# Hybrid decoder step on 8 cores: a split first weight load, filler matmuls, and a new instruction order around the sample rows and the pass change

## What is computed

```python
xn = rmsnorm(h, g_mix); z = xn @ w_in          # x_a | B_a | C_a | u | v | g_a | g_b
y_a = (B_a * dwconv3(C_a * x_a)) @ w_out_a     # mixer A
v = rmsnorm(gelu(v), g_v); s = tril(W_s[g]) v + b_s[g]   # in chunks of 128 positions
y_b = (gelu(u) * s) @ w_out_b                  # mixer B
h += (sigmoid(g_a) * y_a + sigmoid(g_b) * y_b) @ w_o
up = dwconv3(rmsnorm(h, g_ffn) @ w_up); h += (gelu(a) * b) @ w_down
h += sigmoid(rmsnorm(h, g_ple) @ w_ple_gate) * (p @ w_ple)
y = rmsnorm(h, g_final)
```

## Time and profile before

| | us |
|---|---|
| median of 3 runs (lowest, highest) | 1170.34 (1170.22, 1171.02) |
| the profiled execution's own time | 1170.05 |
| its span on the slowest core (core 2) | 1168.3 |
| spans of the 8 cores | 1163.5 to 1168.3 |
| PE busy in the span | 1124.1 (96%) |
| DVE, ACT, POOL busy | 609.8, 384.7, 341.8 |
| granted TensorE clock of the 8 cores, share of full | 0.996 to 0.998 |
| DMA queues: share of 16 engines | 40.9% (weights), 11.3% (the rest) |

### The profile page before, as it was taken

The page is one execution under the profiler, slowest core; times in us unless marked ns, Lnnn a source line. Parts: engine busy times, 40 slices in busy tenths (PEclk is TensorE's granted clock), DMA queues, the critical chain, the costliest instruction groups (busy, mean ns, idle before and its releaser), DMA issues.

```text
span 1168.3 us, 18289 instructions; the slowest of 8 cores (1163.5 to 1168.3 us)
## 1 busy us (share of the span) xinstructions
PE 1124.1 (96%) x6425; PEld 574.5 (49%) x6520; DVE 609.8 (52%) x668; ACT 384.7 (33%) x649; POOL 341.8 (29%) x451
## 2 busy tenths in 40 slices
PE   4999999999999999999899999999999999999996
PEld 2444454444444444443446666666644444444443
DVE  3267662123687776124615866322267888871247
ACT  3622221111354444014772223112133444430134
POOL 2411113222234434114832010222223333330144
PEclk9999999999999999999999999999999999999998
DMA  7983642544844333358699355244377343343443
GB/s 185 183 158 72 111 71 46 80 83 78 145 93 72 73 73 72 62 92 192 196 195 233 63 116 90 37 73 73 72 127 127 73 73 73 73 90 64 79 102 129
DMA packets 58585, 119.77 MB, mean 103 GB/s; under 512 B 33264, under 2 KB 34032, under 8 KB 55936
## 3 DMA queue, kind: packets, MB, share of 16 engines
q0 software_dynamic: 20112, 82.85, 40.9%
q1 hardware_dynamic: 38240, 35.58, 11.3%
q10 hardware_dynamic: 144, 0.17, 0.1%
HBM read 184.14 MB, written 9.95 MB: 166 GB/s over the span
## 4 chain that ended last, share of the span: by engine, by line
PE 88%; POOL 3%; issue 2%; DVE 2%; DMA 2%; ACT 1%; DVEq 0%; POOLq 0%; ACTq 0%; SPq 0%
PE pq L322 88%; POOL s_wd L335 2%; DMA s_ring<-wpk 1%; DVE s_wd L338 1%; ACT s_xnb L329 1%; POOL s_st_r L335 1%; POOL s_st_ss L335 1%; DMA s_h<-x 1%; ACT s_wd L329 0%; DVE s_h L338 0%; PE pq L326 0%; POOL s_R L335 0%; DVE s_xnb L510 0%; DVE s_xnb L338 0%; DVE s_xn L335 0%
## 5 line engine op out<-in xcount | busy, mean ns | idle before, releaser
L322 PE MATMUL pq<-s_xn,s_ring 128*128 128x512 bf16 (+3 forms) x3693 | 658.1, 334 | 4.2 <-DVE s_wd L338 0.8
L322 PEld LDWEIGHTS pq<-s_xn,s_ring 128*128 128x128 bf16 x3744 | 335.6, 98 | 313.2 <-issue 2.0
L338 DVE SCALAR_TENSOR_TENSOR s_wd<-pq,s_cst,s_wd 128x1023 f32<-128x1023 f32 (+1 forms) x176 | 225.2, 1282 | 63.1 <-ACT s_carry_f L332 53.8
L335 POOL TENSOR_TENSOR s_R<-s_wd 128x1024 bf16<-128x1024 f32 (+3 forms) x84 | 146.3, 1742 | 357.9 <-DVE s_wd L338 166.6
L322 PE MATMUL pq<-s_ring,s_R 128*128 128x512 bf16 x936 | 206.9, 379 | 2.7 <-DVE s_wd L338 1.4
L338 DVE SCALAR_TENSOR_TENSOR s_wd<-s_wd,pq 128x512 f32<-128x512 f32 (+4 forms) x98 | 66.7, 681 | 193.2 <-PE pq L322 170.4
L329 ACT ACTIVATE s_wd<-pq 128x512 f32<-128x512 f32 (+4 forms) x138 | 78.4, 568 | 240.1 <-PE pq L322 238.7
L329 ACT ACTIVATE s_wd<-pq,s_cst 128x1024 f32<-128x1024 f32 x88 | 98.1, 1114 | 165.5 <-PE pq L322 165.5
L322 PEld LDWEIGHTS pq<-s_ring,s_R 128*128 128x128 bf16 x960 | 93.2, 98 | 112.5 <-issue 1.8
L322 PE MATMUL pq<-s_R,s_ring 128*128 128x347 bf16 (+3 forms) x875 | 125.1, 292 | 0.3
L322 PE MATMUL pq<-s_ring,s_xn 128*128 128x512 bf16 (+1 forms) x514 | 119.6, 383 | 5.3 <-DMA s_ring<-wpk 3.3
(11 more groups left out here) (81 smaller groups left out, 483.6 us busy)
## 6 DMA issues: line engine op xcount, KB each, us to landing
s_ring<-wpk POOLq DMA_DIRECT2D x110, 512.0 KB, 8.9
s_ring<-wpk POOLq DMA_DIRECT2D x20, 1024.0 KB, 10.0
s_h<-x SPq DMA_DIRECT2D x16, 512.0 KB, 16.1
y<-s_wd SPq DMA_DIRECT2D x15, 512.0 KB, 2.7
s_R<-x SPq DMA_DIRECT2D x8, 512.0 KB, 9.2
s_ring<-wpk POOLq DMA_DIRECT2D x4, 768.0 KB, 7.2
s_gbc<-g_v SPq DMA_DIRECT2D x2, 512.0 KB, 15.0
s_gbc<-g_ffn SPq DMA_DIRECT2D x2, 512.0 KB, 6.3
```

The source lines that it names most:

```text
L322: P.op("pe", lambda e: e.matmul(out, lhsT=lhsT, rhs=rhs, start=start, stop=stop), reads=reads, writes=writes, signal=signal)
L335: P.op(eng, lambda e: e.tensor_tensor(out=out, in0=in0, in1=in1, op=op), reads=reads, writes=writes)
L338: P.op("dve", lambda e: e.scalar_tensor_tensor(out=out, in0=in0, scalar=scalar, in1=in1, op0=op0, op1=op1), reads=reads, writes=writes)
```

## The change

1. Item 0 is loaded by two DMAs of half its columns. `v0a` is the first half. Tiles 2 and 3 of h wait for v0a alone (before: tile 2 for tile 0, tile 3 for the whole item, tile 4 too), and each later tile t for tile t-2. Item 1 is released behind the rstd of tile 4, not 5.
2. `warm(18)` and `warm(28)`: 46 matmuls of 128x128 on constants, into bank 5, whose result nobody reads, around the transposes of tile 1.
3. The setup of the spatial weights (`setup_spatial`) runs on POOL, not on DVE.
4. In the second pass the pairs of banks of the output projection are shifted, so tile 0 takes banks 4 and 5, tile 7 banks 0 and 1.
5. In the second pass's first pair of up-projection groups S1 stands behind `(1, "a", 1)`.
6. In the down-projection the sample rows' matmuls of the last item stand ahead of the last four tiles.
7. In the last stage `y_rstd` of tile t-1 stands behind the add of tile t on POOL; the item for the second pass is released at t = 1, not 2; behind the loop, the transposes of x tiles 5, 6 and 7 stand behind `B_mm` of tiles 1, 3 and 4 (before: ahead of 1, 2 and 4), and the last `y_sq` behind `B_mm(1, 0, 0)`.

```diff
+                if i == 0:
+                    for q, wr in ((0, ["v0a"]), (1, res)):
+                        P.dma("pool", (lambda e, q=q: e.dma_start(out=land[:, q * 2048:(q + 1) * 2048], in_=wsrc[:, q * 2048:(q + 1) * 2048])),
+                              "wv0a" if q == 0 else f"wr{s}", writes=wr)
...
-        for t, after in ((2, [("h", 0)]), (3, v0r), (4, [("h", 1)] + v0r), (5, [("h", 2)]), (6, [("h", 3)]), (7, [("h", 4)])):
+        for t, after in ((2, ["v0a"]), (3, [("h", 1), "v0a"]), (4, [("h", 2)]), (5, [("h", 3)]), (6, [("h", 4)]), (7, [("h", 5)])):
...
-            TTT("dve", WsT[:], ws[:, 0:1024].rearrange("p (j t) -> p j t", j=8), bc_mid(tr[:, 0:128], 8), ALU.mult, [wsr, trr], ["WsT"])
+            TTT("pool", WsT[:], ws[:, 0:1024].rearrange("p (j t) -> p j t", j=8), bc_mid(tr[:, 0:128], 8), ALU.mult, [wsr, trr], ["WsT"])
...
-            if t == 5:
+            if t == 4:
                 R.limit = 2
                 R.prefetch()
...
+        def warm(n):
+            pw, pwr = psR.at(5)
+            for q in range(n):
+                MM(pw[:, 0:128], ones[:], idb[:], True, True, ["ones", "idb"], pwr, q == n - 1)
+
         heads[0].tp()
+        warm(18)
         heads[1].tp()
+        warm(28)
         heads[2].scale()
...
-                pO, pOr = psR.at(2 * (t % 3), 2)
+                pO, pOr = psR.at(2 * ((t + (2 if samp else 0)) % 3), 2)
...
-                    order = [(0, "a", 0), "T6", (0, "b", 0), (1, "a", 0), "T7", "S0", "S1", (0, "a", 1), (0, "b", 1), "E0",
-                             (1, "a", 1), (1, "b", 0), (1, "b", 1), "E1"]
+                    order = [(0, "a", 0), "T6", (0, "b", 0), (1, "a", 0), "T7", "S0", (0, "a", 1), (0, "b", 1), "E0",
+                             (1, "a", 1), "S1", (1, "b", 0), (1, "b", 1), "E1"]
...
+                        if samp and grp == 1 and q == 2:
+                            sample_H(pHs, pHsr, wv_, wvr, lo, hi, half)
...
-                if plus:
-                    normed.append(y_sq(plus.pop()))
+                prev = plus.pop() if plus else None
+                if prev:
+                    normed.append(y_sq(prev))
                 STT(tg[:, 0:D], tg[:, 0:D], 1.0, pE, ALU.add, ALU.mult, [tgr] + pEr, [tgr])
                 TTT("dve" if samp and t >= 4 else "pool", tg[:, 0:D], tg[:, 0:D], h[:, t, :], ALU.add, [tgr, ("h", t)], [tgr])
                 plus.append((t, tg, tgr))
+                if prev:
+                    y_rstd(normed[-1])
...
-                if pss == 0 and t == 2:
+                if pss == 0 and t == 1:
                     R.limit = len(ITEMS) + 2
                     R.prefetch()
...
-                A_push(1, 7)
-                normed.append(y_sq(plus.pop()))
+                A_sq(7)
+                nxt[6].scale()
                 B_mm(1, 0, 8)
-                pipeA.scale()
+                y_out(normed.pop(0))
                 B_mm(1, 0, 0)
+                last = y_sq(plus.pop())
+                y_rstd(last)
+                nxt[7].scale()
                 for t in range(1, 8):
-                    if pipeA.q and t in (1, 2, 4):
-                        pipeA.pop_tp()
-                    if normed:
-                        y_out(normed.pop(0))
                     B_mm(1, 0, t)
+                    if t == 1:
+                        nxt[5].tp()
+                    if t == 3:
+                        nxt[6].tp()
+                        y_out(last)
                     if t == 4:
+                        nxt[7].tp()
```

More of the change, by code:

```diff
@@ L530, in push @@
                 tn.sq()
+                tn.rstd()
                 self.scale()
@@ L619, in build_program @@
             heads[t].sq()
-            if t == 5:
+            heads[t].rstd()
+            if t == 4:
                 R.limit = 2
@@ L912, in build_program, with sample_H @@
                 store(cfs_d[:, :], sfT[:].rearrange("p s r c -> p (s r c)"), "stcfs", ["sfT"] + [("sfTo", c) for c in range(44)])
+            def sample_H(pHs, pHsr, wv_, wvr, lo, hi, half):
+                for i in range(4):
+                    for c in range(lo, hi):
+                        MM(pHs[:, i * NS:(i + 1) * NS], wv_[:, c - lo, i * 128:(i + 1) * 128], act[:, c, 1024:1040],
+                           i == 0 and c == 0, i == 3 and c == 21, wvr + [("act", "s")],
+                           pHsr + (["R1busy"] if c == 21 else []), c == hi - 1)
+                if hi == 22:
+                    hh = hsf[:, half * 64:(half + 1) * 64]
+                    STT(hh, pHs[:, 0:64], 2.0, hh, ALU.mult, ALU.add, pHsr + ["hs"], ["hs"])
             for half in range(2):
@@ L932, in build_program @@
                                     pipe.push(TileNorm(h[:, t, :], ("h", t), 128, t * 128, t, 2))
-                        if samp and grp == 1:
-                            for i in range(4):
-                                for c in range(lo, hi):
-                                    MM(pHs[:, i * NS:(i + 1) * NS], wv_[:, c - lo, i * 128:(i + 1) * 128], act[:, c, 1024:1040],
-                                       i == 0 and c == 0, i == 3 and c == 21, wvr + [("act", "s")],
-                                       pHsr + (["R1busy"] if c == 21 else []), c == hi - 1)
-                            if q == 2:
-                                hh = hsf[:, half * 64:(half + 1) * 64]
-                                STT(hh, pHs[:, 0:64], 2.0, hh, ALU.mult, ALU.add, pHsr + ["hs"], ["hs"])
+                        if samp and grp == 1 and q < 2:
+                            sample_H(pHs, pHsr, wv_, wvr, lo, hi, half)
                         if pss == 0 and half == 0:
@@ L1023, in build_program, with A_sq @@
             normed = []
+            nxt = []
+            def A_sq(t):
+                nxt.append(TileNorm(xst[t], ("xst", t), 128, t * 128, t, 0, dma=False, eng="act"))
+                nxt[t].sq()
+                nxt[t].rstd()
             for t in range(8):
@@ L1063, in build_program @@
                 if pss == 0 and t > 0:
-                    A_push(1, t - 1)
-                    if len(pipeA.q) > 2:
-                        pipeA.pop_tp(psR.at(7) if t < 5 else None)
+                    A_sq(t - 1)
+                if pss == 0 and t > 1:
+                    nxt[t - 2].scale()
+                if pss == 0 and t > 2:
+                    nxt[t - 3].tp()
                 if samp:
```

19 lines of the change are left out of this document (8 added, 11 removed).

## The result

The forecast was 1163.0 us, faster. Measured: **1183.95 us** median of 4 runs (1182.61 to 1186.26) against 1170.68 us for the kernel before; the ratio is 1.0115, 95% interval 1.0101 to 1.0129. The change is slower by 1.2%. In all that follows the ratio is the number to trust: the medians also hold executions, left out of the ratios, in which the cores of one or both dies ran at a lower granted clock, 0.81 at the lowest.

The account below looks back on a forecast made before the run. PE was taken as the bound, busy 1124.1 of 1168.3 us, leaving 44 us idle to win. Terms -1.5 - 4.4 + 0.3 - 1.2 - 0.4 = -7.2 us against 1170.05 gave 1163.0 us, forecast's own range 1161 to 1165, overall 1160.8 to 1167.0.

Parts of the forecast that it names:

- The start, -1.5: First pass, loads of h and item 1: second half of v starts at 37.6 instead of 39.05 us, -1.5 us.
- The filler: Matmuls ahead of v of tile 0: that v may run at the upper clock, 1.89 us instead of 3.57; counted 0.
- I charge little for item 1 starting while tiles 6 and 7 are in flight: Start: h loads with a weight item behind them still took 7.1 us at the median, so sharing costs little.
- Rival (a): Start: item 1 and h of tiles 6 and 7 share by halves, +1.0 instead of -1.5, 1165.5 us; chance 0.12.
- The last stage of the first pass, -4.4: With rstd behind the add, the ring of waits opens and PE's lost time behind the first transposes goes, -4.4 us.
- both fit into 4.76, so PE becomes the bound: First pass, last stage: per turn ACT's 4.25 us and POOL's about 4 fit into PE's 4.76.
- so I charge nothing: First pass, last stage: the weight item loaded one turn earlier takes from the x loads, wanted one per turn; 0.
- Spatial setup, 0: Setup moved to POOL: about 4 us there, first reader a stage later, so 0; uncovered, +4.
- bank shift, +0.3: Second pass, output projection to up-projection: -0.8 at tile 0, +1.05 from a new 1.7 us wait on tile 7; +0.3.
- S1, -1.2: Second pass, up-projection: S1 moved back clears the way for the convolution and fits into a 0.80 us wait, -1.2 us.
- Second pass, last stage, -0.4: Tile 0's 1.31 us wait on the sample bank goes; the matmuls behind begin at 1124.6 instead of 1125.0, -0.4 us.
- (d): Rival for all stages: PE loses clock everywhere at once, each 1% less costing 11 us; 1% gives 1174; chance 0.04.

Follow-up runs that it names:

- c_last: The kernel before with only the new last stage of the first pass, without early release of the gate items: 1172.31 us, ratio 1.0014.
- b_rstd: The kernel before with only the rstd pair moved behind the GpSimd add in the second pass's last stage: 1174.12 us, ratio 1.0033.
- c_rel: The change with second-pass rstd pair first, item 1 behind tile 5, first-pass gate items released ahead of tile 7's last-stage work: ratio 1.0000.
- a_rstd: The change with the rstd pair again ahead of the GpSimd add in the second pass's last stage: 1178.45 us, ratio 1.0071.

## Why the prediction was wrong, point by point

**The start, -1.5.** The filler did what was said (v of tile 0 in 1.89 us, from 15.27 on core 7), tiles 2 to 6 came at most 1.8 us later than forecast, most of them sooner. The step that failed is "I charge little for item 1 starting while tiles 6 and 7 are in flight": with it four of eight cores reached the first mark at 312.6 to 314.7 us, 5.0 to 7.1 us behind the latest core before. I had said that tile 7 has its issue ahead of item 1 ("tiles 6 and 7 have 3 us ahead of item 1"), and the change's own chain of loads lets it fall behind: tile 7 waits for tile 5, item 1 only for tile 4's rstd, and item 1 went out first on four of eight cores. Rival (a) had the place and the sign, but a fraction of the size: halves instead of most of the engines' time, and neither PE's lost clock nor the four items behind tile 7's rstd. With that fault mended the start gave nothing that can be measured, so -1.5 was wrong too: it was worked from core 2, where the second half of v started at 39.05 us, among the latest. Its 37.6 is about what the eight cores had on the mean before the change (37.5), and tile 7 landed no sooner than before.

**The last stage of the first pass, -4.4.** It measured -1.5 to -1.9 at its best. The 5.13 us between adds was one turn of several, 4.74 to 5.25 long on core 2 and 5.0 on the mean. And the step "both fit into 4.76, so PE becomes the bound" failed: on core 1 the four turns behind the first transposes took 5.63, 4.76, 5.01 and 4.76 us, 20.16 in all, against 20.41 before and the 19.04 of the forecast. So the opened ring gave 0.25 us; the other 1.3 came behind the loop, where the transposes moved. The first turn still hangs on ACT (PE waits 0.71 us). The third turn's 0.25 us is a pow that met VectorE's scaling, where the prediction counted GpSimd at the lengths of the earlier trace rows. And 0.7 us remain ahead of tile 7's transposes. And "so I charge nothing" for the ring left out the other item: the one for the second half of v, issued 0.7 to 1.0 us later in the stage while PE comes 1.5 us sooner. On its cores it cost up to 4.7 us, 2.7 to 3.0 of them wait, the rest mostly matmuls at the lower clock. This alone turned the part's sign (c_last).

**Spatial setup, 0; bank shift, +0.3; S1, -1.2.** The setup took 9.8 us on GpSimd (100.3 to 110.1 on core 1), not the 4 of the prediction, but PE had no wait over 0.2 us there from 50 to 300 us, so the 0 stands. The new wait of 1.7 was 1.54. S1's -1.2 didn't come: its matmuls were cover for the copy of tile 7's transposes, and 1.09 us of wait took their place. From v to the down-projection, banks and S1 together are +0.13 instead of -0.9.

**Second pass, last stage, -0.4.** The 1.31 us went, 0.91 and 0.5 came: +0.3 by itself. But the rstd pair behind the add, which I had weighed only for the first pass, stands in a loop that serves both. There it measured +2.5 to +4.6 us on every core of b_rstd and of the change, the largest loss that no core escapes. No rival held it: (d) had the sign, but a clock that falls everywhere; here it falls for a few microseconds behind many of the long waits.

**The sum.** -7.2 was forecast; on quiet core 1 it was +4.1, on the slowest +12.7. The rest of the distance is a maximum over eight cores, of which each could draw a late load at two places, core 7 here at a third; the prediction worked its sum mostly on one core. The 44 us of idle PE time that it began from were 39, since its trace lacked matmul records; no term of the sum hangs on it.

**Open.** With the new start the time from pT of tile 0 to the first transposes of x was longer (median over the cores 16.5 to 18.0 us in eight of ten such traces, 15.2 to 16.1 in the seven with the old one), and the x loads landed later: in c_rel, core 2, against 6.3/9.2/12.9 on this core before,

```profile
DMA to landing us min/median/max: 8.7/16.5/17.8
```

It eats what the start wins. The two exceptions, 15.7 and 16.0, are the change and a_rstd, where a late tile 7 threw the cores up to 10 us out of step at the first mark. That cores in step ask for x at the same moment would fit, but no run tested it.

## What to carry to other kernels

- Where a loop's order is changed for one use of it, read every instruction that shares a queue with it in the other use; and of two loads that can be issued together, issue first the one that is waited for first, by a clear lead (here 2 us was enough, 0.1 us was not).
- Before a GpSimd operation of some length is moved, look at what VectorE does with two SBUF operands at that moment: a short product on the critical path can wait for the whole of it.
- When PE is made faster ahead of a prefetch, the prefetch has less time: compare the moment of issue, not its place in the program, with the moment of need, on the slowest core.
